# Packing the first layer of a mixture of experts by halves of its columns

## The reference, cut to what matters

```python
def moe_ffn(u, router_w, router_b, w1, b1, w2, b2):
    logits = (xf @ router_w + router_b)                  # 256 tokens, 32 experts
    top_val, top_idx = lax.top_k(logits, 4)
    gate = jax.nn.softmax(top_val, axis=-1)
    ...
    def expert_block(args):
        tok, e = args
        hcat = xf[tok] @ w1[e] + b1[e]                   # 1024 -> 2048
        h_glu = jnp.minimum(hcat[:, :1024], 7.0)
        h_lin = jnp.clip(hcat[:, 1024:], -7.0, 7.0)
        act = h_glu * jax.nn.sigmoid(1.702 * h_glu) * (h_lin + 1)
        return act @ w2[e] + b2[e]                       # 1024 -> 1024
    ...
    # the rows of each token are summed with its gates as weights
```

## Time and profile before

| | |
|---|---|
| Median of 3 runs | 2051.35 us (2049.64 to 2051.96) |
| Span of the profiled execution | 2047.8 us |
| TensorE busy | 1938.0 us, 95% |
| TensorE weight loads | 1281.3 us, 63% |
| VectorE busy | 915.7 us, 45% |
| ScalarE busy | 644.4 us, 31% |
| DMA | 589.90 MB, mean 288 GB/s |

### The profile page before, as it was taken

The page is one execution under the profiler, slowest core; times in us unless marked ns, Lnnn a source line. Parts: engine busy times, 40 slices in busy tenths (PEclk is TensorE's granted clock), DMA queues, the critical chain, the costliest instruction groups (busy, mean ns, idle before and its releaser), DMA issues.

```text
span 2047.8 us, 26788 instructions
## 1 busy us (share of the span) xinstructions
PE 1938.0 (95%) x11046; PEld 1281.3 (63%) x11046; DVE 915.7 (45%) x1565; ACT 644.4 (31%) x1086; POOL 10.6 (1%) x24
## 2 busy tenths in 40 slices
PE   8999999999998999999999999999999989899888
PEld 8979998979996677877898333333333333333332
DVE  6877677977766337456656211111111111111112
ACT  5565556565556324355644100000000000000001
POOL 0000000010000000000000000000000000000000
PEclk9999999999999999999999999999999999999999
DMA  8345544445546644031448999999999999999997
GB/s 316 118 165 199 185 165 168 153 180 207 185 165 267 244 172 171 32 122 43 157 176 356 372 421 433 433 432 431 430 431 432 433 432 433 430 431 431 432 432 309
DMA packets 45164, 589.90 MB, mean 288 GB/s; under 512 B 5328, under 2 KB 6032, under 8 KB 10960
## 3 DMA queue, kind: packets, MB, share of 16 engines
q1 hardware_dynamic: 43296, 583.09, 69.7%
q0 software_dynamic: 1488, 5.28, 0.9%
q10 hardware_dynamic: 288, 0.24, 0.0%
HBM read 587.54 MB, written 1.05 MB: 287 GB/s over the span
## 4 chain that ended last, share of the span: by engine, by line
PE 73%; DMA 20%; DVE 3%; ACT 3%; issue 1%; SPq 0%; DVEq 0%; ACTq 0%
PE psum L2113 46%; PE psum L2589 19%; DMA slots<-exp_w_dram 11%; DMA work<-exp_w_dram 7%; PE psum L2534 3%; PE psum L2715 3%; DVE split_weights L1635 0%; DMA slots<-ada_w_dram 0%; DVE work L1461 0%; ACT work L959 0%; ACT split_rows L988 0%; ACT split_weights L1145 0%; DVE work L1779 0%; PE psum L2133 0%; PE psum L2260 0%
## 5 line engine op out<-in xcount | busy, mean ns | idle before, releaser
L2589 PE MATMUL psum<-slots,work 128*64 128x512 f32 x2304 | 516.4, 600 | 52.4 <-DMA slots<-exp_w_dram 44.2
L2113 PE MATMUL psum<-split_rows,split_weights 128*128 128x256 f32 (+1 forms) x3792 | 506.3, 295 | 6.4 <-DVE split_rows L1402 3.4
L2113 PEld LDWEIGHTS psum<-split_rows,split_weights 128*128 128x128 f32 x3792 | 483.9, 192 | 31.0 <-issue 11.0
L2589 PEld LDWEIGHTS psum<-slots,work 128*64 128x64 f32 x2304 | 166.8, 138 | 364.8 <-issue 329.6
L1423 DVE TENSOR_TENSOR split_weights<-slots,split_weights 128x1024 fp32r<-128x1024 f32 x180 | 219.5, 1223 | 121.3 <-ACT split_weights L1003 120.4
L1003 ACT ACTIVATE split_weights<-slots 128x1024 fp32r<-128x1024 f32 x180 | 190.4, 1062 | 184.8 <-PE psum L2113 164.8
L2113 PE MATMUL psum<-split_weights,split_rows 128*128 128x512 f32 x1008 | 233.5, 391 | 0.0
L2113 PEld LDWEIGHTS psum<-split_weights,split_rows 128*128 128x128 f32 x1008 | 188.3, 188 | 41.9 <-issue 3.3
L2078 DVE TENSOR_SCALAR work<-psum 128x512 f32<-128x512 f32 x32 | 22.0, 687 | 388.3 <-PE psum L2589 388.3
L2589 PE MATMUL psum<-work 128*64 128x512 f32 x768 | 173.0, 603 | 17.1 <-DMA work<-exp_w_dram 17.1
L1331 ACT ACTIVATE work<-work 128x512 f32<-128x512 f32 x32 | 20.2, 631 | 475.4 <-DVE work L2078 475.4
(11 more groups left out here) (284 smaller groups left out, 1360.4 us busy)
## 6 DMA issues: line engine op xcount, KB each, us to landing
slots<-exp_w_dram SPq DMA_DIRECT2D x68, 4096.0 KB, 29.8
work<-exp_w_dram SPq DMA_DIRECT2D x23, 4096.0 KB, 29.8
slots<-w_in_dram SPq DMA_DIRECT2D x56, 1024.0 KB, 6.0
slots<-ffn_up_dram SPq DMA_DIRECT2D x44, 1024.0 KB, 4.8
slots<-ada_w_dram SPq DMA_DIRECT2D x24, 1024.0 KB, 8.6
slots<-ffn_down_dram SPq DMA_DIRECT2D x20, 1024.0 KB, 4.8
slots<-w_out_dram SPq DMA_DIRECT2D x12, 1024.0 KB, 4.8
slots<-exp_w_dram SPq DMA_DIRECT2D x4, 2048.0 KB, 8.6
```

The costliest lines, as they stand in the source:

```text
L2113: return nc.tensor.matmul(out_, lhsT, rhs, start=first, stop=last)
L2589: return nc.tensor.matmul(b[rows, :], lhs[:, rows], rhs, start=first, stop=last, skip_group_check=True)
```

## The change

What it does:

- `w1` is packed by `pack_first`. A slot now holds half of the rows (four chunks `k`) over half of the columns of GLU and of LIN. Slots 1 and 2 fill GLU 0 and LIN 0, slots 3 and 4 fill GLU 1 and LIN 1. The bias matmuls follow each pair of banks.
- The spread's transposes and the first hidden half's transposes stand between the third and the fourth slot. The second half's transposes stand before the sixth slot, directly before the wait for their copy. OUT is in banks 6 and 7 now, AT2 1 in bank 4.
- `start_sum(0)` is in the router's part, before `start_sum(1)`. `add_biases` runs in the last pair, before the second layer, and the transposed gates share bank ST there.
- The first pair's fifth slot is loaded in four rows and its sixth in two halves; `first_rows_free` counts used rows of the first and second slot. The last pair's third to sixth slots are all loaded in four rows.

```diff
-MOE_BANKS = [..., ("ST", 0, 6), ("AT2", 0, 7), ("OUT", 0, 4), ("OUT", 1, 5), ("AT2", 1, 6)]
+MOE_BANKS = [..., ("ST", 0, 6), ("AT2", 0, 7), ("OUT", 0, 6), ("OUT", 1, 7), ("AT2", 1, 4)]
...
                     elif part == "first" and n == 4:
+                        to, src = (v.rearrange("p (x k n) -> p x k n", x=2, k=4) for v in (to, src))
+                        for k in range(3):
+                            sp.wait_ge(first_rows_free, k + 1)
+                            sp.dma_start(to[:, :, k, :], src[:, :, k, :]).then_inc(first_rows_loaded, 16)
+                        sp.wait_ge(expert_slot_free, 6 * it + (n + 1))
+                        sp.dma_start(to[:, :, 3, :], src[:, :, 3, :]).then_inc(loaded, 16)
+                        continue
+                    elif part == "first" and n == 5:
                         to, src = (v.rearrange("p (x h n) -> p x h n", x=2, h=2) for v in (to, src))
-                        sp.wait_ge(first_half_free, 1)
-                        sp.dma_start(to[:, :, 0, :], src[:, :, 0, :]).then_inc(first_half_loaded, 16)
+                        sp.wait_ge(first_rows_free, 4)
+                        sp.dma_start(to[:, :, 0, :], src[:, :, 0, :]).then_inc(first_rows_loaded, 16)
...
-                    if part == "last" and n >= 3:
-                        n_k = 2 if n == 3 else 4
-                        to, src = (v.rearrange("p (x k n) -> p x k n", x=2, k=n_k) for v in (to, src))
-                        for k in range(n_k):
+                    if part == "last" and n >= 2:
+                        to, src = (v.rearrange("p (x k n) -> p x k n", x=2, k=4) for v in (to, src))
+                        for k in range(4):
...
                     if part == "first":
-                        evac(("gT", 0), l, gT[0:N_EXP, :], take(act, ("gT", 0), l)[0:N_EXP, 0:T])
...
                         nc.scalar.activation(sig[n], glu[n], ACT.Sigmoid, scale=ALPHA).then_inc(sig_ready, 1)
-                    evac(("ST", 0), it, spread_T, take(act, ("ST", 0), it)[:, 0:T])
-                    evac(("AT2", 0), it, flat(actT[:, 0:4, :]), take(act, ("AT2", 0), it))
+                        if n == 0:
+                            b = take(act, ("ST", 0), it)
+                            if part == "last":
+                                nc.scalar.activation(gT[0:N_EXP, :], b[0:N_EXP, T:2 * T], ACT.Copy)
+                            evac(("ST", 0), it, spread_T, b[:, 0:T])
+                            evac(("AT2", 0), it, flat(actT[:, 0:4, :]), take(act, ("AT2", 0), it))
...
+                start_sum(0)
                 start_sum(1)
...
+                    for q in range(4):
+                        n, kh = divmod(q, 2)
+                        banks = [("GLU", n), ("LIN", n)]
+                        if q == 1:
+                            after_evacuation(pe, ("G", 1), it)
+                        by_rows = q >= 2 and part == "last"
+                        wt = expert_slot(pe, it, odd, q, 4, not by_rows)
+                        if part == "first" and q == 2:
+                            pe.wait_ge(third_part_loaded, 16)
+                        for k in range(4):
+                            if by_rows:
+                                pe.wait_ge(last_rows_loaded[q, k], 16) if k < 3 else expert_slot(pe, it, odd, q, 4)
+                            for i, key in enumerate(banks):
+                                if kh + k == 0:
+                                    fill(pe, key, it)
+                                for xx in (0, 1):
+                                    ins = part_mm(psum[:, bank_of(key), :], xx, xgT[:, 4 * kh + k, :],
+                                                  wt[xx](k, 512 * i, 512 * i + 512), kh + k == 0)
+                                    if xx and (k, i) == (3, 1):
+                                        ins.then_inc(expert_slot_free, 1)
+                                    elif part == "first" and xx and i and (q, k) in ((0, 0), (0, 1), (0, 2), (1, 1)):
+                                        ins.then_inc(first_rows_free, 1)
+                        if kh == 1:
+                            ...
+                            for key, c0 in zip(banks, (512 * n, D + 512 * n)):
+                                done(nc.tensor.matmul(psum[:, bank_of(key), :], pick_e[0:2 * N_EXP, :],
+                                                      b1_split[0:2 * N_EXP, c0:c0 + 512], start=False, stop=True,
+                                                      skip_group_check=True), key)
+                        if q == 2:
+                            b = fill(pe, ("ST", 0), it)
+                            for t in range(TT):
+                                ins = nc.tensor.transpose(b[:, t * P:(t + 1) * P], pick_gated[:, t, :], ident)
+                            if part == "last":
+                                pe.wait_ge(gates_ready, 1)
+                                for t in range(TT):
+                                    ins = nc.tensor.transpose(b[0:N_EXP, T + t * P:T + (t + 1) * P], gate_row[:, t, :], ident)
+                            done(ins, ("ST", 0))
+                            hidden_transposed(0)
+
+                    if part == "last":
+                        after_evacuation(pe, ("ST", 0), it)
+                        add_biases()
...
                         if q:
+                            hidden_transposed(1)
                             after_evacuation(pe, ("AT2", 1), it)
...
-                            if (q, k, n) == (0, 2, 0):
-                                hidden_transposed(1)
...
+def pack_first(a):
+
+    a = np.asarray(a)[0].reshape(PAIRS, 2, 2, 4, P, 2, 2, 512)
+    return np.ascontiguousarray(a.transpose(0, 6, 2, 4, 1, 3, 5, 7)).reshape(PAIRS, 4, P, 4 * HALF)
```

More of the change, by code:

```diff
@@ L2570, in second @@
                 done(mm(b[:, 0:N_EXP], ones, chosen[:, 1, :], False, True), ("CN", 0))
[L2571 to L2577, removed]
                 def add_biases():
-                    after_evacuation(pe, ("gT", 0), l)
                     pe.wait_ge(b2_scaled, 1)
@@ L2599, in pair @@
                         done(ins, ("G", g))
[L2601 to L2611, removed]
-                                 [(k, i) for i in range(4) for k in (0, 1)])
-                        for k, i in order:
-                            if by_rows and i == 0:
-                                pe.wait_ge(last_rows_loaded[q, k], 16) if k == 0 else expert_slot(pe, it, odd, q, 2)
-                            key, n, c0 = banks[i]
-                            end_of_bank = q == 3 and k == 1
-                            if q + k == 0:
-                                fill(pe, (key, n), it)
-                            for xx in (0, 1):
-                                ins = part_mm(psum[:, bank_of((key, n)), :], xx, xgT[:, 2 * q + k, :],
-                                              wt[xx](k, c0, c0 + 512), q + k == 0, end_of_bank)
-                                if xx and end_of_bank:
-                                    done(ins, (key, n))
-                                elif xx and (k, i) == (1, 3):
-                                    ins.then_inc(expert_slot_free, 1)
-                                elif part == "first" and xx and (q, k, i) == (0, 0, 3):
-                                    ins.then_inc(first_half_free, 1)
-                        if q == 0 and part == "first":
-                            gates_turned()
-                        if q == 2:
-                            pe.wait_ge(picks_ready, it + 1)
-                            if part == "first":
-                                pe.wait_ge(b1_split_ready, 2)
-                            for key, n, c0 in banks:
-                                nc.tensor.matmul(psum[:, bank_of((key, n)), :], pick_e[0:2 * N_EXP, :],
-                                                 b1_split[0:2 * N_EXP, c0:c0 + 512], start=False, stop=False, skip_group_check=True)
@@ L2640, in pair @@
-                    b = fill(pe, ("ST", 0), it)
-                    nc.tensor.transpose(b[:, 0:P], pick_gated[:, 0, :], ident).then_inc(expert_slot_free, 1)
-                    done(nc.tensor.transpose(b[:, P:T], pick_gated[:, 1, :], ident), ("ST", 0))
-                    if part == "first":
-                        start_sum(0)
-                        add_biases()
                     def hidden_transposed(n):
@@ L2660, in pair @@
                         wt = expert_slot(pe, it, odd, 4 + q, 4, not by_rows)
-                        if part == "first" and q == 0:
-                            pe.wait_ge(first_half_loaded, 16)
+                        if part == "first":
+                            pe.wait_ge(first_rows_loaded, 48 + 16 * q)
                         if q:
+                            hidden_transposed(1)
                             after_evacuation(pe, ("AT2", 1), it)
```

18 lines of the change are left out of this document (11 added, 7 removed).

## The result

The changed kernel is slower: 2055.66 us median of 11 runs (2049.59 to 2059.38) against 2051.35 us median of 11 runs of the kernel before (2048.75 to 2053.86). The ratio is 1.0021, with a 95% interval of 1.0013 to 1.0030. The prediction was 2048.9 us with a range of 2045.3 to 2052.2: wrong in sign and outside its range.

A forecast was written before the change was run, and what follows sets the result against it. Transfers were taken to bound the flat stage, TensorE's chain the end. With the stream 1.6 us earlier, layer two would end at 2034.0 against 2036.54; 2.5 us off 2051.35 gave 2048.9 us, range 2045.3 to 2052.2.

The forecast's parts named there:

- The router's 0.97 us: In the router's part, start_sum(0) ahead of start_sum(1) delays the logits' matmul and everything in the first pair by 0.97 us.
- the closed hole: Near 1193 us, at the second pair's fifth slot: its issue moves to 1189.4, closing a hole that lost 1.2 us.
- the stream's gain of 1.6 us: At the second pair's fifth slot, data goes on at 1193.1 instead of 1194.7; bounds of the gain 0.8 to 2.6.
- the price of the 4 KB pieces: In slots loaded by rows, 410 against 431 GB/s costs the last pair's third slot 0.5 us.
- the last bytes: At the stream's end, the final data was forecast to land at 2031.7 us, against 2032.56 before.
- rows 2.41 us apart: In the last pair, the spacing at which the rows of its slots were taken to land.
- only one row is left of the third slot when it has landed: In the last pair, third slot's last row lands at 2002.8; TensorE then finishes that slot's products at 2004.7.
- a mere exchange (0.69 for 0.75): On TensorE, a 0.69 us stall for the first hidden half goes; one of 0.75 for the second half comes.
- of 58.3 us, TensorE needs 53.8: In the flat stage, TensorE has 53.8 us of work per 58.3 us pair, so nothing there eats the stream's gain.
- The 3.6 us of bias sums: In the last pair before layer two, 8 records take 3.6 us; TensorE falls behind the rows, which cover them, not fully.
- The end gains nothing: Rival: bias sums and longer stall (3.6 + 1.36) delay TensorE, or first hole stays; near 2050.8, no change; chance 0.12.
- Each transfer pays for its start: Rival: 5 more transfers in the last pair's third and fourth slots each idle 2.2 us; 2058.8; chance 0.10, shared.

The follow-up runs named there:

- a7_whole_slots: a3_both with the last pair's third and fourth slots each loaded in one piece: 2049.84 us, ratio to the kernel before 0.9996.
- a3_both: The changed kernel with bias sums and gate transposes back in the first pair and second hidden half transposed mid fifth slot: 2050.05 us, ratio to before 1.0004.
- the control: The changed kernel run once more with no edit, beside the kernel before: 2056.45 us, ratio to before 1.0023.
- a2: The changed kernel with the second hidden half transposed after two rows of the fifth slot again: 2050.27 us, ratio to before 1.0002.
- b1: The kernel before with the second hidden half transposed behind the wait for the sixth slot: 2053.26 us, ratio to before 1.0011.
- a1: The changed kernel with the gates' transposes and the bias sums in the first pair again: 2051.05 us, ratio to before 1.0001.
- g3: a3_both taken again unchanged, as the control of a later group: 2050.06 us, ratio to the kernel before 0.9996.
- b2: The kernel before with the bias sums moved to the last pair, behind the spread's transposes: 2053.57 us, ratio to before 1.0013.
- a6: The changed kernel with the four bias sums replaced by products over 128 rows of identity and x, biases left out: 2053.65 us, ratio to before 1.0013.
- g2: a3_both with the bias sums replaced by products over 128 rows of identity and x, biases left out: 2049.10 us, ratio to the kernel before 0.9991.
- g1: a3_both with the four bias sums spread out, one behind each row of the first pair's fifth slot: 2049.63 us, ratio to the kernel before 0.9997.
- g4: g1 with start_sum(0) moved back into the first pair, before the first spread sum: 2050.81 us, ratio to the kernel before 1.0001.

## Why the prediction was wrong

**The start was right.** The router's 0.97 us (0.86 measured), the closed hole, the stream's gain of 1.6 us, the price of the 4 KB pieces, and the last bytes to 0.2 us were as worked out. The changed kernel's window in the stage of the pieces:

```profile
1992.00:2022.00 30.00, 30.00 (x137) 1.00 1.03 409
```

The Trainium skill, "DMA: Bandwidth & Descriptors", Specifications, has it that pieces of 512 B reach line rate. By it these pieces would have been free; the traces of both kernels disagree (409 and 410 against 430 to 432 GB/s), and a7_whole_slots most directly.

One slip stands in the sum: rows 2.41 us apart would be 435 GB/s, above the 410 that it uses beside them. In a3_both, where TensorE waits for the rows, they come about 2.5 us apart. Since TensorE was not waiting in the changed kernel, the slip had no part in the miss.

**The step that failed** is "only one row is left of the third slot when it has landed, 2002.8 + 0.14 + 1.77 = 2004.7". It took for granted that TensorE would be waiting at the third slot of the last pair and take its rows as they came. In the changed kernel that slot's products end at 2012.0. The 7.3 us between are three things:

- 4.4 us: TensorE was not there. From the sixth slot's landing at 1973.18 it needs 0.14 + 7.02 + 3.6 + 3.6 + 13.9 + 0.65 us (the slot, sums, gather, two slots, biases) and reaches the third slot at 2002.1 at best, then has all 7.0 us of it to do: 2009.1. The rows could win nothing there. The wait of 0.98 us before the third slot in the kernel before said how little room there was; I read only the chain from 2003.91 on.
- 1.5 us: the transposes of the second hidden half and their copy stand behind the wait for the sixth slot. I costed the stall as a mere exchange (0.69 for 0.75), and hid it in the flat stage with "of 58.3 us, TensorE needs 53.8". In the last-but-one pair there is no later transfer to hide it.
- 1.4 us: the spell of half clock on the sixth slot, which no term of the sum had. It was more in other executions (2.4 us in the control's profile).

From there my sum was near: 29.3 us to the end of layer two were forecast, 27.9 measured. The 3.6 us of bias sums were in the sum, but as the price of a TensorE that had caught up. In truth they came in full on top of a chain that bound the end, and in some executions with a second spell on them (3.4 us more in the control's profile).

**The comparison.** The profiled end of layer two moved from 2036.54 to 2039.88, 3.3 us. From start to start in the two timelines the terms are: sums +3.6, gate transposes +0.2, the second half's wait and copy +0.9 in the last pair, first spell +1.4, divided biases +0.2, against the gap before the third slot -1.05, and the copy of the first hidden half that is now covered -1.8. The earlier landing and its 1.5 us of serial work together are near 0 (1974.83 against 1974.89, -0.06). The sum is the measured 3.3, to rounding. The runs' medians differ by 4.3 us. The profiled execution has the highest granted clock of the eleven (0.986 against 0.980 to 0.985), and the control's profile shows what more half clock can add at the end: 1.1 us in the first spell and 3.4 in a second. How much of that is in the median is not measured.

**The rivals.** "The end gains nothing" named the right things, the bias sums and a longer stall, and was priced as no change because I still let the start's gain come through. "Each transfer pays for its start" was wrong: the queue ran at 409 GB/s over 1992 to 2022, and at 393 in the window before its last. That the time went up, the side on which this rival stood, had another reason, which the rivals did not have at this size: a TensorE that was behind for the whole end.

**What stays open.** That the late second half brings more half clock is shown by the granted clock of all runs of a2 and b1. That a spell goes with the bias sums stands in single profiles only. Ten profiles have the sums over 32 rows one behind the other. Six of them have a spell during or right behind them (the control, a1, a2, a7, g3, and b2, there behind a wait of 0.69 us), four have none (before, the first of the changed kernel, a3, b1). None of the four with 128 rows or with the sums spread out has one (a6, g2, g1, g4). That leans towards the 32 rows in a row as the cause, and does not show it. Why half clock comes in some executions and pairs and not in others is not known. No version beats the kernel before by what can be measured; g2, whose interval ends at 0.9999, leaves the biases out.

## What to carry to other kernels

Where transfers set the pace for hundreds of microseconds, the last of them still leave a tail that the compute engine may bound: follow that engine back from the end until it really waits, before you price anything by landings. Here the last real wait was 0.98 us, ahead of the third slot. Work placed behind the wait for the last transfers is paid in full there, though the same instructions cost the stream nothing in the earlier pairs. Loading by rows wins only if the reader is there before the last row is in.

## What the hardware showed that was not expected

In the changed kernel the waits of a pair gather before the sixth slot (2.81 us, four transposes, then 0.78 us). The granted clock falls to half there for about 3 us (0.55 and 0.60 over 4 us), again and again with the pairs' period. In the kernel before the waits are spread over the slots, at most 1.97 us each in this stretch, and its last 400 us of products ran without a spell. In both kernels earlier pairs have such spells too (five of them before, between 1372 and 1620 us). Moving four transposes changed the mean granted clock from about 0.982 to 0.989. A spell can also come with no idle time before it: in g3_both_again at 1160 us, in a1_bias_sums_first and a7_whole_slots at 1163 us, in the control at 2024 us and in a2_second_hidden_mid at 2021 us, in each case during or right behind the eight records of the bias sums, with TensorE busy for tens of microseconds before.
